# A two-path hybrid trunk step: sample inputs broadcast by transfers, the first chunk after a norm ordered by input tile, and a pair of heads moved into the step of two state reads

## The chip, the cores and the metric

One core of one Trainium2 chip runs the whole program as one launch. The metric is the device time of an execution in microseconds (us), the median of the runs. Engines: PE is TensorE, DVE is VectorE, ACT is ScalarE, POOL is GpSimd (here it only issues transfers), SP is SyncE (it issues the weight loads). All arithmetic is in fp32.

## What is computed

The reference runs one trunk of two layers for a prompt of 256 tokens and for 8 samples that each add one token; the kernel carries both as 264 columns. Layer 0 mixes by stick-breaking attention and retention, layer 1 by a gated state-space scan; after each mixer comes a layer norm, then a convolutional feed-forward part, then a layer norm. The parts that matter here, cut to their core:

```python
def _layer_norm(x, g, b):
    mu = jnp.mean(xf, axis=-1, keepdims=True)
    var = jnp.mean(jnp.square(xf - mu), axis=-1, keepdims=True)
    return ((xf - mu) * lax.rsqrt(var + LN_EPS) * g + b)
...
def _ssd_scan(x, dt, a, bm, cm, d_skip, h0):
    ...
    contrib = jnp.einsum('bcjgs,bcjge,bcjgep->bcgeps', bc, to_end, xf)
    def step(h, inp):
        return h * cd[..., None, None] + ct, h
    ...
    y = y + jnp.einsum('bcigs,bcige,bcgeps->bcigep', cc, jnp.exp(cum), h_start)
    y = y + d_skip.astype(jnp.float32)[:, :, None] * xf
```

For a sample the scan is one step: its state of a group (128 rows of the state by 8 heads x 64 = 512 channels) is multiplied by a decay for each head, and the outer product of B (128 values) and dt * x (512 values) is added; the new state is then read with C.

## The kernel before

**Products.** The weights come in 473 chunks of 1 MB (4 input tiles by 4 output tiles of 128 x 128), one after another through all phases. SP loads a chunk to `raw`; ACT copies it, rounded, to `hi` (line 553); DVE makes the rest, `lo = raw - hi` (line 563), each two chunks ahead of PE (`LOOK`); PE then makes three matmuls for each of the 16 blocks (lines 653 to 655: hi x xh, hi x xl, lo x xh), 48 for a chunk, each with 264 moving columns, into four accumulators `acc`. This stream of matmuls runs through the whole program; everything else that PE does is put between its pieces.

**Norms.** Three of four layer norms (l = 0, 1, 2) are followed by a phase that multiplies their result (up0, bc, up1). In the last chunk ahead of a norm PE sums, and then runs 12 unneeded matmuls (line 2381). DVE (`norm`) forms mean and variance, then centres four input tiles at once (`center`, line 1789, 128 x 1056), inverts the root that ACT made of the variance (lines 1172, 1810), and for each tile of 264 columns scales (`scale_tile`, line 1797) and, once ACT has rounded the tile to `xh` (line 1188), makes the rest `xl` (`low_tile`, line 1802). This is repeated for the four groups q of four tiles. PE starts chunk 0 of the next phase tile by tile (`x_first`, `x_lo`) with the output tile n as outer loop and the input tile k as inner loop; chunks 1, 2 and 3 wait for all four tiles of group 1, 2 and 3.

**The scan** runs beside the 64 chunks of the phase "ssd". Each chunk has four steps of 12 matmuls; a group g of 8 heads takes 28 steps (r = 0 to 27, 7 chunks), 8 groups in all, and tables give the step at which each piece of work is put behind the 12 matmuls, on PE and in the same order on DVE, ACT and POOL. Each engine works strictly in its order. The pieces are:
- at r = 22 PE turns the inputs of the samples of the next group (`group_samples`), DVE multiplies them by dt into `xtmp` (line 2046, 8 rows of 512), ACT rounds them and DVE makes the rest (line 2051), both into rows of `xdr`;
- `spread` at `SPREAD_AT` (r = 0, 2, 5, 7, 10, 12, 15, 17), one for each sample b: one matmul of 512 columns against a column of a selector (line 2426) that copies the row of sample b to 128 partitions of the bank `bank_spread`. DVE then adds it times B to the state (`renew`, line 1960). One bank serves all: the next spread waits for `state_new`, the renewal before;
- `read_state` for two samples at r = 5, 10, 15 and 20 (line 2440, 16 records for 8 matmuls of 8 x 128);
- `pair_heads` for two heads of the prompt at `PAIR_AT` = 4, 9, 14, 19 (lines 2459, 2461), which DVE adds to the result in the same step (line 1968). `DECAY_AT` and `WEIGHT_AT`, the steps of the preparations on ACT and DVE, are computed from `PAIR_AT`;
- at r = 20 also `group_cb` (lines 2485, 2486), at r = 26 and 27 turns and products of the prompt's inputs (lines 2103, 1985).

**POOL** issues the transfers of the scan in one fixed order. A unit u is the states of two samples in one group (512 KB, 32 units in all); for each u: load the state of u + 2 (line 843, which waits for the store of u - 1 to land and for its reads), load the decay rows of u + 2, broadcast to 128 partitions (line 835, which waits for ACT to have used the buffer), wait for both renewals of u, store the state (line 861).

## Time and profile before

| | |
|---|---|
| time before, median of 3 runs | 3062.95 us (3060.9 to 3064.45) |
| the profiled execution: its time, its span from first to last instruction | 3062.5 us, 3060.7 us |
| busy share of the span: PE, DVE, ACT, POOL | 99%, 65%, 53%, 4% |
| share of PE, DVE and ACT in the chain of work that ended last | 92%, 5%, 1% |
| HBM traffic over the span | 195 GB/s |
| mean granted TensorE clock | 0.996 of full |

Times in a trace are from the span's start. A row of the timeline gives the start, the time from the start of the first to the end of the last of its instructions, engine, line, operation and tiles, and in brackets the idle time of the engine ahead of it and what ended it. Matmuls overlap: each stands with some 0.28 us, but the next one starts 0.12 us later, so the cost of something on PE is read from starts. fp32 matmuls that are not of the rounded kind leave two records each.

### The profile page before, as it was taken

The page shows a single profiled execution, that of the slowest core. Times are in us where ns is not written, and L with a number is a line of the kernel's source. Part 1 is how long each engine was busy: PE and PEld are TensorE (multiplying, and loading weights), DVE is VectorE, ACT ScalarE, POOL GpSimd, SP SyncE. Part 2 cuts the span into 40 slices and gives each one's busy share as a digit, 9 for nine tenths or more (in the row PEclk, how much of TensorE's full clock was granted, in tenths as well). Part 3 has the DMA queues.
Part 4 walks back from the last instruction along what each step waited for, and adds up shares of the span by engine and source line. Part 5 has one row for each costly group of instructions (what it writes and reads, how often), then busy time and mean ns, then how long its engine had stood idle before and what let it go on. Part 6 is the DMA issues. An engine that isn't in the chain of part 4 may idle for free.

```text
span 3060.7 us, 60293 instructions
## 1 busy us (share of the span) xinstructions
PE 3016.8 (99%) x25089; PEld 2948.4 (96%) x25089; DVE 1985.3 (65%) x2512; ACT 1628.1 (53%) x1744; POOL 125.0 (4%) x222
## 2 busy tenths in 40 slices
PE   9999999999999999999999999999999999999997
PEld 9999899999999999999999999999999999999997
DVE  5455454677655666667758888777686566556665
ACT  4435575545444445445556767775454444445453
POOL 1010100000000000000000111100000000000000
PEclk9999999999999999999999999999999999999998
DMA  7565667544445445544456776665444544455452
GB/s 273 183 239 205 225 218 278 193 159 167 165 180 199 169 178 205 191 164 179 179 218 216 240 243 230 235 210 194 179 162 179 196 175 172 182 202 182 178 192 84
DMA packets 94523, 598.07 MB, mean 195 GB/s; under 512 B 11120, under 2 KB 11136, under 8 KB 33312
## 3 DMA queue, kind: packets, MB, share of 16 engines
q1 hardware_dynamic: 68688, 498.17, 44.0%
q0 software_dynamic: 25680, 97.69, 9.2%
q8 instruction: 115, 1.88, 0.2%
q14 instruction: 40, 0.33, 0.0%
HBM read 558.66 MB, written 37.15 MB: 195 GB/s over the span
## 4 chain that ended last, share of the span: by engine, by line
PE 92%; DVE 5%; ACT 1%; issue 1%; DMA 1%; DVEq 0%; POOL 0%; POOLq 0%; SPq 0%; ACTq 0%
PE acc L653 29%; PE acc L654 28%; PE acc L655 28%; DVE lo L563 1%; PE aux L2103 1%; PE aux L2426 1%; PE aux L2459 1%; PE aux L2440 1%; DVE x L1789 1%; DVE xl L1802 1%; DVE x L1797 1%; ACT xh L1188 0%; ACT hi L553 0%; PE aux L2188 0%; DMA x<-xsave 0%
## 5 line engine op out<-in xcount | busy, mean ns | idle before, releaser
L653 PE MATMUL acc<-xh,hi 128*128 128x264 f32 x7552 | 2174.8, 288 | 10.0 <-DVE lo L563 5.0
L654 PE MATMUL acc<-xl,hi 128*128 128x264 f32 x7552 | 2146.5, 284 | 0.0
L655 PE MATMUL acc<-xh,lo 128*128 128x264 f32 x7552 | 2139.0, 283 | 0.0
L653 PEld LDWEIGHTS acc<-xh,hi 128*128 128x128 f32 x7552 | 1422.9, 188 | 26.6 <-issue 13.9
L654 PEld LDWEIGHTS acc<-xl,hi 128*128 128x128 f32 x7552 | 1423.1, 188 | 4.2
L655 PEld LDWEIGHTS acc<-xh,lo 128*128 128x128 f32 x7552 | 1419.9, 188 | 0.0
L563 DVE TENSOR_TENSOR lo<-raw,hi 128x2048 fp32r<-128x2048 f32 x473 | 1077.7, 2287 | 381.2 <-ACT hi L553 380.5
L553 ACT ACTIVATE hi<-raw 128x2048 fp32r<-128x2048 f32 x473 | 897.6, 1907 | 492.6 <-DMA raw<-in_w 324.0
L552 ACT ACTIVATE xh<-pj 128x1056 fp32r<-128x1056 f32 x144 | 156.0, 1083 | 340.2 <-PE acc L655 279.6
L560 DVE TENSOR_TENSOR xl<-pj,xh 128x1056 fp32r<-128x1056 f32 x144 | 180.7, 1255 | 203.5 <-ACT hi L553 200.2
L1512 DVE SCALAR_TENSOR_TENSOR stage<-acc,par,stage 128x255 f32<-128x255 f32 x352 | 168.9, 480 | 23.1 <-DVE stage L1512 21.9
L901 ACT ACTIVATE stage<-acc,par 128x264 f32<-128x264 f32 x176 | 100.1, 571 | 133.8 <-PE acc L655 129.5
L935 ACT ACTIVATE pj<-acc 128x264 f32<-128x264 f32 x56 | 21.7, 389 | 78.7 <-PE acc L655 78.6
L1960 DVE SCALAR_TENSOR_TENSOR x<-aux,pj,x 128x512 f32<-128x512 f32 x64 | 47.8, 747 | 20.6 <-PE aux L2426 20.6
L911 ACT ACTIVATE small<-small 128x1 f32<-128x1 f32 x48 | 9.8, 203 | 89.5 <-DVE stage L1512 74.0
L1608 DVE SCALAR_TENSOR_TENSOR x<-x,aux 128x256 f32<-128x256 f32 x64 | 24.1, 418 | 50.2 <-PE aux L2188 50.2
L1845 DVE TENSOR_TENSOR pj<-stage 128x528 f32 (+1 forms) x44 | 31.2, 709 | 38.3 <-ACT stage L1199 38.3
L1428 DVE SCALAR_TENSOR_TENSOR x<-x,acc 128x264 f32 (+1 forms) x48 | 19.5, 426 | 43.9 <-PE acc L655 43.9
L1933 DVE SCALAR_TENSOR_TENSOR pj<-stage,par,pj 128x255 f32<-128x255 f32 (+2 forms) x96 | 46.2, 481 | 2.3
L808 POOL DMA_DIRECT2D out_fconv<-pj x2 | 1.1, 550 | 1049.4 <-DVE stage L1512 1049.4
L1951 DVE TENSOR_TENSOR x<-x,extra 128x512 f32<-128x512 f32 x64 | 43.7, 683 | 0.0
L1188 ACT ACTIVATE xh<-x,par 128x264 fp32r<-128x264 f32 x48 | 23.5, 512 | 30.7 <-DVE x L1797 30.7
(284 smaller groups left out, 1609.3 us busy)
## 6 DMA issues: line engine op xcount, KB each, us to landing
raw<-in_w SPq DMA_DIRECT2D x473, 1024.0 KB, 4.9
x<-in_ssm POOLq DMA_DIRECT2D x32, 512.0 KB, 4.4
out_ssms<-x POOLq DMA_DIRECT2D x32, 512.0 KB, 5.1
x<-in_ret POOLq DMA_DIRECT2D x16, 512.0 KB, 5.4
out_rets<-x POOLq DMA_DIRECT2D x16, 512.0 KB, 3.9
x<-in_ck POOLq DMA_DIRECT2D x16, 512.0 KB, 3.9
x<-in_cv POOLq DMA_DIRECT2D x16, 512.0 KB, 5.6
pj<-cumd POOLq DMA_DIRECT2D x32, 256.0 KB, 5.7
```

What stands on the lines that cost most here:

```text
L552: act.activation(xh[:, CK * s:CK * s + CK, :], src[:, CK * kc:CK * kc + CK, :], ACT.Copy)
L553: act.activation(hi[:, ph.hi(j), :], raw[:, r, :], ACT.Copy).then_inc(hi_done, 1)
L560: dve.tensor_tensor(xl[:, CK * s:CK * s + CK, :], src[:, CK * kc:CK * kc + CK, :], xh[:, CK * s:CK * s + CK, :].bitcast(F32), ALU.subtract)
L563: dve.tensor_tensor(lo[:, r, :], raw[:, r, :], hi[:, ph.hi(j), :].bitcast(F32), ALU.subtract).then_inc(lo_done, 1)
L653: pe.matmul(out, hi[:, s, w], xh[:, a, :], start=kc == 0 and k == 0, stop=False)
L654: pe.matmul(out, hi[:, s, w], xl[:, a, :], start=False, stop=False)
L655: m = pe.matmul(out, lo[:, r, w], xh[:, a, :], start=False, stop=kc == ph.kc - 1 and k == CK - 1)
L901: a(dst(q, n), acc[n][:, 0:T], ACT.Identity, bias=col(bias), scale=col(w))\
L1512: ins = stt(y[:, k:SEQ], h[:, 0:SEQ - k], one(w[:, width - 1 - k, :], n), y[:, k:SEQ], ALU.mult, ALU.add)
L1933: stt(y[:, k:SEQ], h[:, 0:SEQ - k], scw[:, 3 - k, t:t + 1], y[:, k:SEQ], ALU.mult, ALU.add)\
L1951: tt(v, v, cdbc[:, 8 * g:8 * g + 8, b].unsqueeze(2).to_broadcast([P, 8, HD]), ALU.mult)\
L1960: stt(v, bank_spread[:, :], pt[:, BM + g, SEQ + b:SEQ + b + 1], v, ALU.mult, ALU.add)\
```

## The change

Three edits. (1) In the scan, PE's 64 spread matmuls, ACT's rounding and DVE's rest of the inputs go. Instead `group_samples` makes four narrow matmuls that put the inputs of the 8 samples in four bands of 32 rows, DVE multiplies 104 rows of 128 by dt, POOL writes the four bands to a small array `xds` in HBM (`inputs_out`) and reads each sample's row of 512 back, broadcast to 128 partitions (`input_load`), into one of two SBUF buffers `xbc`; `renew` reads that buffer in place of the PSUM bank. (2) After the norms 0, 1 and 2 DVE centres the first four tiles one by one, and PE works chunk 0 with the input tile as outer loop; the first pass through the phase's loop is written out. (3) `PAIR_AT` moves by one step, to the steps of the reads.

```diff
-PAIR_AT = (4, 9, 14, 19)
+PAIR_AT = (5, 10, 15, 20)
...
-        xdr = hi[:, NHI - 1, 1536:2048]
+        xbc = [hi_end[:, 1536:2048], extra[:, 0:512]]
...
+            def first_chunk():
+
+                s, r = ph.hi(0), ph.raw(0)
+                pe.wait_ge(lo_done, ph.chunk0 + 1)
+                for k in range(CK):
+                    if k < CK - 1:
+                        pe.wait_ge(R["x_first"], (CK - 1) * (split - 1) + k + 1)
+                    else:
+                        pe.wait_ge(R["x_lo"], XB * split + 1)
+                    for n in range(CN):
+                        if k == 0:
+                            pe.wait_ge(drained, 4 * ph.panel0 + n + 1)
+                        w = slice((k * CN + n) * P, (k * CN + n + 1) * P)
+                        out = acc[n][:, 0:T]
+                        pe.matmul(out, hi[:, s, w], xh[:, k, :], start=k == 0, stop=False)
+                        pe.matmul(out, hi[:, s, w], xl[:, k, :], start=False, stop=False)
+                        m = pe.matmul(out, lo[:, r, w], xh[:, k, :], start=False, stop=False)
+                m.then_inc(used, 1)
...
-                    if pb == 0 and split is not None and (kc or not split):
+                    if pb == 0 and split is not None and (begun or not split):
...
+            elif split:
+                first_chunk()
+                body(Step(0), begun=True)
...
+            def inputs_out(g):
+
+                pool.wait_ge(R["misc_free"], MISC["st", g] + 1)
+                for t in range(4):
+                    pool.dma_start(d["xds"][NB * g:NB * g + NB, t * P:t * P + P], xtmp[32 * t:32 * t + NB, :])\
+                        .then_inc(R["xds_out"], 16)
+
+            def input_load(s):
+
+                if s % NB == 0:
+                    pool.wait_ge(R["xds_out"], 64 * (s // NB + 1))
+                if s >= 2:
+                    pool.wait_ge(R["state_new"], s - 1)
+                pool.dma_start(xbc[s % 2].unsqueeze(1), d["xds"][s:s + 1, :].partition_broadcast(P))\
+                    .then_inc(R[f"xbc_in{s % 2}"], 16)
...
+            inputs_out(0)
+            input_load(0)
+            input_load(1)
...
+                if u % 4 < 3:
+                    input_load(2 * u + 2)
                 pool.wait_ge(R["state_new"], 2 * (u + 1))
                 pool.dma_start(d["ssms"][u], hbuf[u % 3]).then_inc(R[f"state_out{u % 3}"], 16)
+                if u % 4 == 3 and u + 1 < units:
+                    inputs_out(u // 4 + 1)
+                    input_load(2 * u + 2)
+                if u + 1 < units:
+                    input_load(2 * u + 3)
...
-                    if r == ST_AT + 1 and -1 <= g < G - 1:
-                        act.wait_ge(R["misc_free"], MISC["st", g + 1] + 1)
-                        if g == -1:
-                            act.wait_ge(R["xdr_zero"], 1)
-                        else:
-                            act.wait_ge(R["spread"], 8 * g + 8)
-                        a(xdr[0:NB, :], xtmp[0:NB, :], ACT.Copy).then_inc(R["xdt_hi"], 1)
...
+                def center_tile(t):
+                    tt(x[:, t, :], x[:, t, :], lsum[:, :], ALU.add).then_inc(R["ln_fin"], 1)
+
+                if l == 3:
+                    center(0)
+                else:
+                    center_tile(0)
...
-                for q in range(XB):
+                scale_tile(0)
+                center_tile(1)
+                dve.wait_ge(R["ln_fin"], 8 * l + 3)
+                scale_tile(1)
+                low_tile(0)
+                center_tile(2)
+                low_tile(1)
+                dve.wait_ge(R["ln_fin"], 8 * l + 4)
+                scale_tile(2)
+                center_tile(3)
+                low_tile(2)
+                dve.wait_ge(R["ln_fin"], 8 * l + 5)
+                scale_tile(3)
+                low_tile(3)
+                for q in range(1, XB):
                     if q == XB - 1:
                         split_lo(dve, lead[l][3][0], Step(0), 3, None)
-                    if q:
-                        center(q)
-                        dve.wait_ge(R["ln_fin"], 5 * l + q + 2)
+                    center(q)
+                    dve.wait_ge(R["ln_fin"], 8 * l + 5 + q)
...
-                dve.wait_ge(R["spread"], 8 * g + b + 1)
+                dve.wait_ge(R[f"xbc_in{b % 2}"], 16 * (4 * g + b // 2 + 1))
                 dve.wait_ge(R["state_aged"], 8 * g + b + 1)
                 v = hbuf[u % 3][:, (b % 2) * 512:(b % 2) * 512 + 512]
-                stt(v, bank_spread[:, :], pt[:, BM + g, SEQ + b:SEQ + b + 1], v, ALU.mult, ALU.add)\
+                stt(v, xbc[b % 2], pt[:, BM + g, SEQ + b:SEQ + b + 1], v, ALU.mult, ALU.add)\
...
-                            dve.wait_ge(R["xdt_lo"], g + 1)
-                            dve.wait_ge(R["xdt_hi"], g + 1)
-                        tt(xtmp[0:NB, :].rearrange("p (h e) -> p h e", e=HD),
-                           dts[0:NB, 8 * g + 8:8 * g + 16].unsqueeze(2).to_broadcast([NB, 8, HD]),
-                           misc[0:NB, :].rearrange("p (h e) -> p h e", e=HD), ALU.mult).then_inc(R["misc_free"], 1)
-                    if r == XT_AT[0] and -1 <= g < G - 1:
-                        dve.wait_ge(R["xdt_hi"], g + 2)
-                        tt(xdr[32:32 + NB, :], xtmp[0:NB, :], xdr[0:NB, :].bitcast(F32), ALU.subtract)\
-                            .then_inc(R["xdt_lo"], 1)
+                            dve.wait_ge(R["xds_out"], 64 * (g + 1))
+                        tt(xtmp[0:104, :].rearrange("p (h e) -> p h e", e=HD),
+                           dts[0:104, g + 1, :].unsqueeze(2).to_broadcast([104, 2, HD]),
+                           misc[0:104, 0:P].rearrange("p (h e) -> p h e", e=HD), ALU.mult).then_inc(R["misc_free"], 1)
...
-            def spread(g, b):
-
-                pe.wait_ge(R["xdt_lo"], g + 1)
-                if g or b:
-                    pe.wait_ge(R["state_new"], 8 * g + b)
-                else:
-                    pe.wait_ge(R["sel_r"], 1)
-                mm(bank_spread[:, :], selr[0:72, b:b + 1].to_broadcast([72, P]), xdr[0:72, :],
-                   start=True, stop=True).then_inc(R["spread"], 1)
...
-                    m = turn(misc[0:NB, t * P:t * P + P], pt[:, XS + 4 * g + t, SEQ:T])
+                    m = mm(misc[32 * t:32 * t + NB, 0:P], pt[:, XS + 4 * g + t, SEQ:T], ident, start=True, stop=True)
...
-                        if r == SPREAD_AT[b]:
-                            spread(g, b)
```

**DVE, norm 0.** The first row below is the variance; line 1789 centres, 1797 scales, 1802 makes the rest. Before:

```order
L1781 SCALAR_TENSOR_TENSOR pj<-aux,pj 128x264
L1789 TENSOR_TENSOR x<-x,lsum 128x1056
L1810 RECIPROCAL pj<-pj 128x264
L1797 SCALAR_TENSOR_TENSOR x<-x,par,pj 128x264 x2
L1802 SCALAR_TENSOR_TENSOR xl<-x,par,xh 128x264
L1797 SCALAR_TENSOR_TENSOR x<-x,par,pj 128x264
L1802 SCALAR_TENSOR_TENSOR xl<-x,par,xh 128x264
L1797 SCALAR_TENSOR_TENSOR x<-x,par,pj 128x264
L1802 SCALAR_TENSOR_TENSOR xl<-x,par,xh 128x264 x2
L1789 TENSOR_TENSOR x<-x,lsum 128x1056
```

The same place now, where line 1847 centres one tile, 1827 four, 1835 scales and 1840 makes the rest:

```order
L1847 TENSOR_TENSOR x<-x,lsum 128x264
L1854 RECIPROCAL pj<-pj 128x264
L1835 SCALAR_TENSOR_TENSOR x<-x,par,pj 128x264
L1847 TENSOR_TENSOR x<-x,lsum 128x264
L1835 SCALAR_TENSOR_TENSOR x<-x,par,pj 128x264
L1840 SCALAR_TENSOR_TENSOR xl<-x,par,xh 128x264
L1847 TENSOR_TENSOR x<-x,lsum 128x264
L1840 SCALAR_TENSOR_TENSOR xl<-x,par,xh 128x264
L1835 SCALAR_TENSOR_TENSOR x<-x,par,pj 128x264
L1847 TENSOR_TENSOR x<-x,lsum 128x264
L1840 SCALAR_TENSOR_TENSOR xl<-x,par,xh 128x264
L1835 SCALAR_TENSOR_TENSOR x<-x,par,pj 128x264
```

Ahead of the second group there are now eleven instructions behind the reciprocal, three more than before, and one narrow centring ahead of it in place of a wide one.

**PE, one group of the scan, r = 0 to 10.** "..." stands for the rows of the stream (lines 653 to 655, now 669 to 671). Before, with spread on line 2426, the pair on 2459 and 2461, the read on 2440:

```order
L2426 MATMUL aux<-hi,selr 128x512
...
L2426 MATMUL aux<-hi,selr 128x512
...
L2459 MATMUL aux<-raw,x 64x256 x2
L2461 MATMUL aux<-raw,x 64x128 x2
L2103 MATMUL aux<-cons,extra 128x128
...
L2440 MATMUL aux<-x,raw 8x128 x8
L2426 MATMUL aux<-hi,selr 128x512
...
L2426 MATMUL aux<-hi,selr 128x512
```

The same steps now, with the turn on line 2160, the read on 2490 and the pair on 2509 and 2511:

```order
L2160 MATMUL aux<-cons,extra 128x128
...
L2490 MATMUL aux<-x,raw 8x128 x8
L2509 MATMUL aux<-raw,x 64x256 x2
L2511 MATMUL aux<-raw,x 64x128 x2
```

The spreads are gone, and the pair has moved from its own step to stand right behind the read.

**POOL, the same part.** Line 855 loads decay rows, 863 a state, 902 stores one, 878 is the new broadcast load:

```order
L902 DMA out_ssms<-x 128x1024
L878 DMA extra<-xds 128x512
L863 DMA x<-in_ssm 128x1024
L855 DMA pj<-cumd 128x512
L878 DMA hi_plain<-xds 128x512
```

Before, the order was the same without the two rows of line 878; at the end of a group four small stores `xds<-pj` now stand ahead of the next two such loads.

## Rows read from the trace of the kernel before

**Rows 1.** A window: length, busy PE, PEld, DVE, ACT, POOL, clock, DMA share, GB/s
```profile
1700.00:1750.00 50.00, 50.00 (x443) 45.95 (x442) 39.97 (x62) 33.84 (x46) 5.88 (x11) 1.00 0.70 248
```

**Rows 2.** Timeline of PE, scan, group 1 and the last read
```profile
1693.38 0.28 PE L655 MATMUL acc<-xh,lo 128*128 128x264 f32 x1
1693.60 0.62 PE L2440 MATMUL aux<-x,raw 128*8 128x128 f32 x16
...
1694.49 0.28 PE L653 MATMUL acc<-xh,hi 128*128 128x264 f32 x1
...
1697.40 0.40 PE L2426 MATMUL aux<-hi,selr 72*128 72x512 f32 x1
1697.64 0.29 PE L653 MATMUL acc<-xh,hi 128*128 128x264 f32 x1
...
1702.45 0.65 PE L2459 MATMUL aux<-raw,x 128*64 128x256 f32 x4
...
1703.25 0.39 PE L653 MATMUL acc<-xh,hi 128*128 128x264 f32 x1
...
1724.16 0.62 PE L2440 MATMUL aux<-x,raw 128*8 128x128 f32 x16
...
1725.39 0.36 PE L653 MATMUL acc<-xh,hi 128*128 128x264 f32 x1
...
2053.27 0.62 PE L2440 MATMUL aux<-x,raw 128*8 128x128 f32 x16
2053.82 0.39 PE L653 MATMUL acc<-xh,hi 128*128 128x264 f32 x1
```

**Rows 3.** Waits of PE: who for whom, total us, times, longest
```profile
PE aux L2103 <- DVE hi_plain L1985: 1.4, 4, 0.4
PE aux L2426 <- DVE x L1960: 1.2, 1, 1.2
```

**Rows 4.** Timeline of DVE in the scan: inputs of group 1, two renewals
```profile
1674.71 0.67 DVE L2046 TENSOR_TENSOR extra<-pj,aux 8x512 f32<-8x512 f32 x1 [1.15 <-PE aux L2103]
...
1685.96 0.74 DVE L1960 SCALAR_TENSOR_TENSOR x<-aux,pj,x 128x512 f32<-128x512 f32 x1
...
1705.99 0.75 DVE L1960 SCALAR_TENSOR_TENSOR x<-aux,pj,x 128x512 f32<-128x512 f32 x1 [0.41 <-PE aux L2426]
```

**Rows 5.** Timeline of POOL, one issue of decay rows in the scan
```profile
1698.63 0.54 POOL L835 DMA_DIRECT2D pj<-cumd  x1 [0.19 <-issue]
```

**Rows 6.** The tile cumd: 33 transfers, from issue to landing
```profile
DMA to landing us min/median/max: 2.0/5.7/8.0
```

**Rows 7.** Timeline of PE behind norm 0: chunks 0, 1 and 3
```profile
692.41 0.36 PE L653 MATMUL acc<-xh,hi 128*128 128x264 f32 x1 [0.41 <-DVE xl L1802]
...
699.77 0.36 PE L653 MATMUL acc<-xh,hi 128*128 128x264 f32 x1 [0.16 <-DVE xl L1802]
...
712.10 0.36 PE L653 MATMUL acc<-xh,hi 128*128 128x264 f32 x1 [0.45 <-DVE xl L1802]
```

**Rows 8.** Timeline of DVE, norm 0
```profile
687.70 1.25 DVE L1789 TENSOR_TENSOR x<-x,lsum 128x1056 f32<-128x1056 f32 x1
688.86 1.80 DVE L1810 RECIPROCAL pj<-pj 128x264 f32<-128x264 f32 x1
690.69 0.90 DVE L1797 SCALAR_TENSOR_TENSOR x<-x,par,pj 128x264 f32<-128x264 f32 x2
691.77 0.49 DVE L1802 SCALAR_TENSOR_TENSOR xl<-x,par,xh 128x264 fp32r<-128x264 f32 x1 [0.18 <-ACT xh L1188]
...
694.47 1.25 DVE L1789 TENSOR_TENSOR x<-x,lsum 128x1056 f32<-128x1056 f32 x1
```

**Rows 9.** Timeline of ACT, norm 0: the root of the variance
```profile
687.81 0.52 ACT L1172 ACTIVATE pj<-pj,small 128x264 f32<-128x264 f32 x1 [1.85 <-DVE pj L1781]
```

**Rows 10.** Two windows in the attention part, columns as in rows 1
```profile
473.00:475.00 2.00, 0.37 (x16) 0.08 (x4) 1.97 (x3) 0.00 (x0) 0.41 (x1) 1.00 1.00 399
477.00:479.00 2.00, 2.00 (x11) 2.00 (x11) 0.00 (x0) 0.92 (x2) 0.53 (x1) 0.50 1.00 348
```

49 lines of the change are left out of this document (27 added, 22 removed).

## The prediction

> **What bounds the kernel now.** I read first the page's busy shares and the chain that ended last (table above): PE is busy 99% of the span and holds 92% of the chain. Then a window in the middle of the scan [rows 1]: PE 50.00 us of 50.00, DVE 39.97, ACT 33.84, the transfer engines at a share of 0.70. So in the scan every nanosecond that PE spends beside the stream of chunk matmuls is paid in full, and DVE and the transfers have some room, of a fifth to a third. Then the starts on PE around each piece of work beside the stream [rows 2], and last the three norms, which are the only places in these phases where PE waits for DVE again and again [rows 7].
>
> **Spreads.** A stream matmul starts 0.12 us after the one before. A spread alone moves the next stream matmul by 0.24 (1697.40 to 1697.64) [rows 2]. A read with a spread behind it costs 1693.38 to 1694.49, 1.11 less the usual 0.12, so 0.99; a read alone costs 0.55 from its start, and 0.10 more because such a block starts 0.22 after the last stream row and not 0.12, so 0.65 [rows 2]. A spread behind a read is thus 0.34. Of 64 spreads 24 stand behind a read (r = 5, 10, 15 in 8 groups) and 40 do not: 24 x 0.34 + 40 x 0.24 = 17.8 us off PE.
>
> **Waits that go with them.** One spread waited 1.2 us for the renewal ahead of it, because one bank serves all; four turns at r = 26 waited 1.4 us together for DVE's products [rows 3], which stand right behind the rest (line 2051) that the change removes. Both go: 2.6 us. I count them whole; the lower end is nothing, if other waits come in their place.
>
> **Pairs.** A pair alone costs 0.80 + 0.10 = 0.90 [rows 2]. No row shows a pair behind a read. The nearest is `group_cb` behind a read, with the same 256 and 128 moving columns: 1.23 + 0.10 = 1.33 for both, so 0.68 for the second piece [rows 2]. I take 0.68, since what is saved is entering and leaving the stream once instead of twice: 32 x 0.22 = 7.0 us. The lower end is nothing saved. The Trainium skill ("TensorEngine Tiling (Array Packing)", Key Properties) speaks against this edit: a change of tiling mode drains the engine, and the read (8 columns wide) and the pair (64 wide) are different modes. By that rule the join saves less than 7.0, perhaps nothing; the row of the read with `group_cb` is also a change of mode and shows 0.68, so I go by the row.
>
> **What PE gets instead.** Eight times four turns become four narrow matmuls. Their nearest row is a read, which has eight such and costs 0.65; four cost between half of that and all of it, and what the turns cost today comes off. I take 0.1 us net for each group, 0.8 us; the ends are -2 and +3 us. The turn that shared the pair's old step now stands alone, which is in the same bounds.
>
> Scan, on PE: -17.8 - 2.6 - 7.0 + 0.8 = -26.6 us.
>
> **The broadcasts by transfer** cost PE nothing while they land in time. POOL's issues take 0.54 us each [rows 5], and a broadcast of 256 KB, like the decay rows, lands 5.7 us after its issue in the median and 8.0 at the most [rows 6]. At the head of a group the inputs are made at 1674.71 and the first renewal runs at 1685.96 [rows 4]: 11.2 us. Needed: 0.3 for the product, 4 x 0.54 for the stores, 2.0 for a small store to land (the least in rows 6 is the one store among them), and 5.7: 10.2. That leaves 1 us in the median, and is 1.3 too late at 8.0. Inside a group the load for an even sample can be issued right behind the decay rows, at 1698.63 + 0.54 = 1699.17, and is wanted at 1705.99 [rows 4, 5]: 6.8 us, against 5.7 and something for standing behind the decay rows. At r = 0 the decay load itself moves one step later with `PAIR_AT`, and takes this load along. So some renewals will be late by 0 to 2 us. What is queued behind them is DVE's own work: the next ageing, a pair's result, and `lo` of a chunk two chunks ahead. DVE has 10 of 50 us free and loses its waits for spreads, so I cost this at 0 for PE; the upper end, 0.4 us in each of 32 units, is 13 us. The 64 loads are 17 MB in some 430 us, 39 GB/s on top of 248 [rows 1], so the share of 0.70 becomes about 0.81; the weights keep their place five chunks ahead.
>
> **The norms.** Here the edit works against itself. DVE, by [rows 8, 9]: the wide centring starts at 687.70 and the reciprocal at 688.86, the first scaling at 690.69, 1.83 after the reciprocal. A narrow centring takes between 0.31 (a quarter of 1.25) and 0.41 (two scalings take 0.90, one 0.49); I take 0.35. It would let the reciprocal start at 688.05, but the root on ACT ends at 687.81 + 0.52 = 688.33. So the first scaling starts at 690.2, 0.5 us earlier. From there to the wide centring of group 1 there were eight instructions in 694.47 - 690.69 = 3.78 us; now there are eleven: 3.28 for the eight at 0.41, 1.05 for three centrings, and 0.9 of waits, mostly of the last rest, which cannot start before 1.08 after its scaling (690.69 to 691.77) as ACT must round between. That is 5.2 to 5.4, so group 1 starts at about 695.55, 1.1 us later than today, and so do groups 2 and 3, which are unchanged. On PE [rows 7]: chunk 0 starts at some 692.1 instead of 692.41 and, with no gaps, is through at 697.9 instead of 699.6. But chunk 1 waits for group 1 today already (0.16 us at 699.77), and chunk 3 for group 3 (0.45 at 712.10). Both now come 1.1 us later: chunk 1 at 700.9, after 2.8 us of idle PE, and chunk 3 at 713.2 (PE by itself would be there at 700.9 + 11.9 = 712.8, so DVE still decides). The gain in chunk 0 is lost in front of chunk 1, and what is left is 1.1 us more for each of three norms: +3.3. Ends: 0 and 1.5 for each.
>
> **The clock.** In the attention part PE was busy for only 0.37 of 2.00 us, and soon after ran at a granted clock of 0.50, 1.2 instead of 2.4 GHz, with 11 matmuls in 2 us where 16 start otherwise [rows 10]. The new idle stretch of 2.8 us behind each norm is longer than that one. A fall costs at least the 0.9 us of work lost in those 2 us, at most perhaps twice that; I take 1.5, of which the 0.4 that chunk 3 has in hand comes off: 1.1 us. I count one fall in three norms, +1.1; ends 0 and 4.5. The Trainium skill ("TensorE: Matmul & The Clock Gate", HAM oscillation) says the same of gaps between bursts of matmuls: the engine returns to half clock. [...]
>
> **The sum.** -26.6 + 3.3 + 1.1 = -22.2 us. The profiled execution has a span of 3060.7 and a time of 3062.5; it becomes 3038.5 and 3040.3. The median of the runs lies 0.45 above its time, so I forecast 3041 us.
>
> **Rivals.**
> - *The join of pair and read saves nothing*, because the engine drains between them: 3041 + 7 = 3048. For it speaks only that no row shows that pair of widths. 0.08.
> - *Late inputs reach PE.* Available times of 6.8 us against 5.7 to 8.0 speak for it, DVE's room against. With a third to all of the 13 us: 3045 to 3054. 0.13.
> - *The norms gain.* If the rests of group 1 came no later than today, chunk 0's earlier end would take off the 0.16 and the 0.45 that PE waits and no clock would fall: -26.6 - 2, so 3035. Against it stands the count of instructions. 0.08.
> - *Slower.* The place is the load for the even samples. It stands behind the state load, which waits for the landing of a store, which waits for the renewal; if a broadcast from the new array lands late, the whole ring turns slower than PE. PE must lose 22 + 6 = 28 us more, 0.9 in each of 32 units, on top of the 6.8 us that are available and some 3 us that DVE and the reads at the end of a unit can take: a landing of 10.7 us in the median decides, against 5.7 (at most 8.0) for the same size today [rows 6]. It would give 3069 and more. 0.06.
> - *The edits cancel, or do not do what they say* (the spreads' columns were hidden, say): within 6 us of 3063. Against it, PE is busy 50.00 of 50.00. 0.04.
>
> The forecast itself has 0.61, with its own range of 3037 to 3045. A measurement of this kernel tells 0.2%, 6 us, from no change. Faster by more: 0.61 + 0.08 + 0.13 + 0.08 = 0.90; within it 0.04; slower 0.06. The range of 3036 to 3050 leaves out the slower case, the cancelling, the worse half of the late inputs and part of the gaining norms.
>
> **What would show it.** Right: no wait of PE for `renew`; a read with its pair from some 1.3 us, at r = 20 some 2.0; chunk 1 behind each norm waiting 2.5 to 3 us for line 1840, chunk 3 some 1.1 us later against the norm's start; renewals waiting 0 to 2 us for the new loads, above all at r = 5; a granted clock of 0.50 behind one norm or two. Wrong: PE waiting in the scan for reads or `lo` behind late renewals; a read with its pair at 1.55; group 1 of a norm starting less than 0.5 us later than now. What would make it wrong most easily is the landing time of the broadcasts, which no row shows for this array.

## The result and the profile after

The changed kernel takes 3072.11 us, the median of 10 runs (3069.87 to 3076.58). The kernel before, run beside it, takes 3064.37 (10 runs, 3060.9 to 3067.14). The ratio is 1.003, with an interval of 1.0022 to 1.0038: slower by 8 us, where 3041 us, 22 less than before, was forecast. The profiled execution has a span of 3072.1, against 3060.7.

From the page of the changed kernel: PE's part of the busy shares, the software queue (packets, MB, share), and three kinds of issues with their size and the median from issue to landing.

```profile
PE 3004.4 (98%) x25064; PEld 2942.2 (96%) x25064; DVE 1978.6 (64%) x2517; ACT 1621.1 (53%) x1733; POOL 174.8 (6%) x317
...
q0 software_dynamic: 31824, 114.61, 11.1%
...
x<-in_ssm POOLq DMA_DIRECT2D x32, 512.0 KB, 6.4
out_ssms<-x POOLq DMA_DIRECT2D x32, 512.0 KB, 7.7
...
pj<-cumd POOLq DMA_DIRECT2D x32, 256.0 KB, 6.4
```

PE lost a percent of its busy share. The window that [rows 1] shows of before, with the same columns, and two short ones behind the first norm:

```profile
700.00:702.00 2.00, 0.21 (x2) 0.24 (x3) 1.82 (x5) 1.71 (x5) 0.00 (x0) 1.00 0.86 287
702.00:704.00 2.00, 2.00 (x11) 2.00 (x11) 1.79 (x4) 1.36 (x4) 0.00 (x0) 0.51 0.58 242
1700.00:1750.00 50.00, 47.49 (x428) 44.12 (x427) 36.57 (x61) 34.17 (x45) 11.17 (x22) 0.97 0.81 266
```

In the scan PE was busy 50.00 of 50.00 before; now it idles for 2.5 of 50 us, and the granted clock of 0.97 says that it ran at 1.2 GHz and not at 2.4 for a part of them. The share of the transfers is 0.81, as forecast. So PE has become a waiting engine. For what, the waits tell (engine, tile and line of the waiting instruction, what released it: us in total, times, the longest). First PE's in the changed kernel, then DVE's:

```profile
PE aux L2509 <- DVE raw L2005: 14.6, 16, 3.4
PE acc L669 <- DVE xl L1840: 8.3, 3, 2.8
PE aux L2490 <- DVE x L2022: 6.6, 9, 1.2
```

```profile
DVE x L2022 <- DMA hi_plain<-xds: 46.9, 13, 6.2
...
DVE x L2022 <- DMA extra<-xds: 14.5, 7, 3.0
```

Before, PE waited 0.2 us for a pair's weights and 1.2 for a renewal in the whole scan; now it waits 14.6 for weights (line 2005), 6.6 for renewals (2022). DVE's renewals wait 61.4 us for the broadcast inputs, 20 times. Only the third group, 8.3 us for `xl`, is of the norms.

One such event from beginning to end. POOL, changed kernel, start and length of each issue (878 is a broadcast of inputs, 855 decay rows, 863 a state load, 902 a state store):

```profile
1690.75 0.57 POOL L878 DMA_DIRECT2D hi_plain<-xds  x1 [4.34 <-DMA xds<-pj]
1691.31 0.55 POOL L878 DMA_DIRECT2D extra<-xds  x1
1691.85 0.53 POOL L863 DMA_DIRECT2D x<-in_ssm  x1
1697.95 0.54 POOL L855 DMA_DIRECT2D pj<-cumd  x1 [5.57 <-ACT raw L1362]
1698.48 0.54 POOL L878 DMA_DIRECT2D hi_plain<-xds  x1
```

DVE, at the other end of the last of these:

```profile
1705.92 0.75 DVE L2022 SCALAR_TENSOR_TENSOR x<-hi_plain,pj,x 128x512 f32<-128x512 f32 x1 [5.09 <-DMA hi_plain<-xds]
...
1707.73 1.51 DVE L1995 SCALAR_TENSOR_TENSOR pj<-stage,par,pj 128x255 f32<-128x255 f32 x3
1709.16 2.29 DVE L563 TENSOR_TENSOR lo<-raw,hi 128x2048 fp32r<-128x2048 f32 x1
1711.37 0.55 DVE L2005 TENSOR_TENSOR raw<-raw 128x384 f32<-128x384 f32 x1
1711.84 0.75 DVE L2022 SCALAR_TENSOR_TENSOR x<-extra,pj,x 128x512 f32<-128x512 f32 x1
...
1714.08 0.55 DVE L2005 TENSOR_TENSOR raw<-raw 128x384 f32<-128x384 f32 x1
```

And PE, with the read on 2490 and the pair on 2509:

```profile
1711.46 0.41 PE L2490 MATMUL aux<-x,raw 128*8 128x128 f32 x8
1712.64 0.41 PE L2490 MATMUL aux<-x,raw 128*8 128x128 f32 x8 [0.77 <-DVE x L2022]
1714.78 0.65 PE L2509 MATMUL aux<-raw,x 128*64 128x256 f32 x4 [1.74 <-DVE raw L2005]
```

The buffer came free when the renewal of 1694.68 had read it, at some 1695.4, but POOL stood from 1692.4 to 1697.95 at the issue of the decay rows, which waits for ACT (5.57 us). The broadcast was issued behind it at 1698.48 and landed 7.4 us later. DVE stood 5.09 us, and when it went on it had its whole order before it: the convolution's products (line 1995), a `lo` of 2.29 us, the pair's first weights, the next renewal and, at 1714.08, the pair's second weights. PE, 6.7 us after the late renewal, waits for the next one (0.77) and then for those second weights (1.74).

The norms behave as forecast. PE at chunk 1 behind norm 0, in the changed kernel (to be set beside [rows 7]):

```profile
698.73 0.28 PE L650 MATMUL acc<-xh,lo 128*128 128x264 f32 x1
701.79 0.36 PE L669 MATMUL acc<-xh,hi 128*128 128x264 f32 x1 [2.78 <-DVE xl L1840]
```

The window above from 702 shows the granted clock of 0.51 behind this idle stretch. The same pair of idle and fall stands behind all three norms (idle 2.78, 2.77 and 2.76 us at 701.79, 1486.91 and 2279.75).

To see where time went I cut each profiled span at PE's starts, at the last unneeded matmul ahead of the norms 0, 1 and 2 and at the start of the scan: up to norm 0, from there to norm 1, the part of dt, the scan with the output projection, and what follows norm 2. The labels are those of the experiments below; each row is one profiled execution. In us, with PE's idle time in the scan:

```
                     span    to n0   n0..    dt     scan   n2..    idle in scan
before              3060.7  691.6   783.4   96.7   691.3  797.7    6.2
changed             3072.1  692.5   785.1   98.3   694.6  801.7   24.0
e1 norms alone      3067.1  691.9   785.3   98.3   691.5  800.1    6.5
e2 pair alone       3060.1  691.7   783.3   96.7   690.7  797.7    6.0
e3 broadcasts alone 3060.1  690.4   783.3   96.7   691.1  798.7   18.5
e5 changed, by ACT  3045.0  692.1   785.1   98.3   670.2  799.4    6.9
e6 e3, by ACT       3051.2  692.5   783.4   96.6   681.0  797.7    9.9
e9 e6 and pair      3038.7  691.0   783.3   96.7   670.0  797.7    6.7
e10 one load first  3054.4  690.4   786.3   97.8   680.1  799.9   12.5
e11 loads unread    3043.7  691.4   784.6   99.5   667.7  800.5    4.7
e12 e3 and pair     3065.6  689.0   783.5   96.7   697.7  798.7   22.7
e13 POOL reordered  3053.5  692.1   784.9   98.1   678.3  800.1   11.8
```

### The profile page after: what moved, and what is told of

It reads as the page before. It is cut to its first block, busy times and chain, and to the rows that moved or that the text cites. A ratio compares the mean times of both kernels' runs of the same rounds, so it can differ in the third digit from the quotient of the medians.

```text
span 3072.1 us, 60119 instructions
## 1 busy us (share of the span) xinstructions
PE 3004.4 (98%) x25064; PEld 2942.2 (96%) x25064; DVE 1978.6 (64%) x2517; ACT 1621.1 (53%) x1733; POOL 174.8 (6%) x317
## 3 DMA queue, kind: packets, MB, share of 16 engines
q0 software_dynamic: 31824, 114.61, 11.1%
## 4 chain that ended last, share of the span: by engine, by line
PE 85%; DVE 6%; DMA 6%; issue 2%; ACT 1%; POOL 0%; DVEq 0%; POOLq 0%; SPq 0%; ACTq 0%
PE acc L669 27%; PE acc L670 27%; PE acc L671 26%; DMA extra<-xds 2%; DMA hi_plain<-xds 1%; DVE lo L563 1%; DMA out_ssms<-x 1%; DMA xds<-pj 1%; DVE x L2022 1%; PE aux L2160 0%; DVE pj L1995 0%; DVE x L2013 0%; DVE raw L2005 0%; PE aux L2245 0%; ACT hi L553 0%
## 5 line engine op out<-in xcount | busy, mean ns | idle before, releaser
L981 ACT ACTIVATE pj<-acc 128x264 f32<-128x264 f32 x56 | 21.7, 389 | 78.7 <-PE acc L671 78.6
L2022 DVE SCALAR_TENSOR_TENSOR x<-hi_plain,pj,x 128x512 f32<-128x512 f32 x32 | 24.0, 750 | 47.2 <-DMA hi_plain<-xds 46.9
L1361 ACT ACTIVATE raw<-pj,x 128x256 f32<-128x256 f32 x64 | 32.2, 503 | 23.7 <-DVE raw L2005 23.7
```

The source lines that it names most:

```text
L2022: stt(v, xbc[b % 2], pt[:, BM + g, SEQ + b:SEQ + b + 1], v, ALU.mult, ALU.add)\
```

## Experiments

Two theories stood at the start. **Late inputs** (theory L of the first texts below): the spreads' time did leave PE, and was lost again because renewals wait for the broadcasts. **Slack** (theory P; later texts name theirs anew): the pair's new step, or the traffic on the transfer engines, is what costs. The edits were first run one by one. A ratio is to the kernel before as run beside that experiment, whose median went from 3063.25 to 3064.53 us, with an interval of 95% behind it; so differences between medians of two experiments are good to about 1 us at best.

**e1_norm**: only the edit at the norms.

```diff
-                center(0)
+                if l == 3:
+                    center(0)
+                else:
+                    center_tile(0)
...
+            elif split:
+                first_chunk()
+                body(Step(0), begun=True)
```

> The kernel before with edit 2 alone (narrow centrings, chunk 0 by input tile). Theory L (the scan loses to late input loads, the norms cost what the trace of the changed kernel shows: 2.8 us of idle PE behind each of three norms and a fall of the clock after each): 5 to 6.5 us slower than before, three falls of the clock. Theory P (the scan loses to the moved pair, with the norms as here): the same. If the norms were not the cause of their share: within 1 us of before.

Measured: 3068.88 us, ratio 1.0021 (1.0012 to 1.003), 5.6 us slower. Windows of e1_norm behind its three norms, columns as above:

```profile
702.00:704.00 2.00, 2.00 (x12) 2.00 (x12) 1.78 (x5) 1.01 (x3) 0.00 (x0) 0.55 0.21 86
1487.00:1489.00 2.00, 2.00 (x13) 2.00 (x12) 1.79 (x4) 1.33 (x4) 0.00 (x0) 0.57 0.43 176
2276.00:2278.00 2.00, 1.78 (x8) 1.81 (x9) 1.96 (x4) 1.36 (x4) 0.00 (x0) 0.50 0.75 315
```

The clock is at half speed, 1.2 GHz, behind every norm: three falls in this execution, where one was counted.

**e2_pair**: only `PAIR_AT`.

```diff
-PAIR_AT = (4, 9, 14, 19)
+PAIR_AT = (5, 10, 15, 20)
```

> The kernel before with edit 3 alone (pair moved into the step of the reads, spreads kept). Theory L: the pair costs about 0.8 behind a read where it cost 0.9 alone, so 0 to 3 us faster, no waits of PE for line 1943. Theory P (the pair in the reads' step has too little time behind its weights on DVE, and this makes PE wait): 10 us slower or more.

Measured: 3062.67 us, ratio 1.0 (0.9991 to 1.001); the scan 0.6 us shorter and no new wait. The pair's step costs nothing as long as the inputs come from spreads.

**e3_bcast**: only the broadcasts, issued by POOL.

```diff
-                        if r == SPREAD_AT[b]:
-                            spread(g, b)
...
+                if u % 4 < 3:
+                    input_load(2 * u + 2)
```

> The kernel before with edit 1 alone (inputs broadcast by transfers). Theory L: PE waits some 15 to 25 us in the scan behind renewals that wait for their load, which eats the 18 us of the spreads: between 5 us faster and 5 us slower than before. Theory P: the loads are hidden, 15 to 20 us faster.

Measured: 3061.86 us, ratio 0.9998 (0.9988 to 1.0007). Renewals wait 33.6 us for loads, 18 times, and PE's first row of waits is

```profile
PE aux L2469 <- DVE raw L1965: 15.4, 10, 2.7
```

So already alone this edit gives back all that the spreads cost, and the row is the pair's weights, not the reads.

**e4_noload**: the changed kernel with 62 of the 64 broadcast loads left out; every renewal reads the inputs of the first two samples, so the states of the samples are other numbers.

```diff
                 if s >= 2:
                     pool.wait_ge(R["state_new"], s - 1)
+                    return
...
-                dve.wait_ge(R[f"xbc_in{b % 2}"], 16 * (4 * g + b // 2 + 1))
+                dve.wait_ge(R[f"xbc_in{b % 2}"], 16)
```

> The changed kernel without 62 of its 64 broadcast loads: every renewal reads the inputs of the first two samples (so the sample states and what follows from them are other numbers); the small stores to HBM and all waits of POOL stay. Theory L: PE's 21 us of waits in the scan and the three falls of the clock there go, 25 us faster than the changed kernel, some 17 us faster than before. Theory P: no more than 5 us faster than the changed kernel, PE still waits for the weights of line 2005.

Measured: 3052.46 us, ratio 0.9969 (0.9956 to 0.9981), 19.7 below the changed kernel, where 25 was expected. The run takes three things away together: DVE's waits, POOL's issues and the traffic. The next ones part them. It also has something of its own: at 2062.56, the end of the scan, PE stands 3.8 us for a `lo`, because DVE has waited 6.06 us for the reload of `xsave`. In e11 below that wait of DVE is 2.35 us, and e11, which does issue the loads, is 7 us faster than e4. So 19.7 is a lower bound of what late loads cost.

**e5_actq**: the changed kernel with the stores of the inputs and the broadcasts issued by ACT, at fixed steps. **e6_actq_old**: the same, but with the norms and the pair's step as before.

```diff
-                pool.dma_start(xbc[s % 2].unsqueeze(1), d["xds"][s:s + 1, :].partition_broadcast(P))\
+                act.dma_start(xbc[s % 2].unsqueeze(1), d["xds"][s:s + 1, :].partition_broadcast(P))\
...
+                    if r == ST_AT + 1 and -1 <= g < G - 1:
+                        inputs_out(g + 1)
+                    if r == ST_AT + 3 and -1 <= g < G - 1:
+                        input_load(NB * (g + 1))
+                        input_load(NB * (g + 1) + 1)
+                    if 0 <= g < G:
+                        for b in range(2, NB):
+                            if r == SPREAD_AT[b - 2] + 1:
+                                input_load(NB * g + b)
```

> The changed kernel with the small stores and the 64 broadcast loads issued by ACT, at fixed steps of the scan (stores at r = 23, the first two loads of a group at r = 25, the others one step after the renewal that frees their buffer), in place of POOL. Theory Q (the loads are late because they stand in POOL's order and its queue, behind state loads and stores of 512 KB): they land 3.5 to 5 us after the issue, PE's waits in the scan fall from 21 to under 8 us, 12 to 20 us faster than the changed kernel. Theory B (the extra traffic itself makes every transfer late): landings stay above 6 us and the time within 5 us of the changed kernel.

> The kernel before with edit 1 alone (norms and the pair's step as before), stores and loads on ACT as in the run before this. Theory Q: the scan as there, and 6 us less for the norms: 15 to 20 us faster than the kernel before. Theory B: within 3 us of the kernel before.

Measured: e5 3046.83 us, 0.9946 (0.9932 to 0.9959), 25.3 below the changed kernel; e6 3051.18 us, 0.9962 (0.9948 to 0.9976), 13 below the kernel before. In e5 renewals wait 6.1 us in 4 places, and the loads land in 5.6 us in the median. Theory Q has the direction and misses its numbers: 3.5 to 5 us for the landing, 12 to 20 us for e5, 15 to 20 for e6. Two windows of e5 in the scan, the first with the columns as above, the second with PE's alone (length, busy PE, clock, DMA share, GB/s):

```profile
1700.00:1750.00 50.00, 47.76 (x440) 44.40 (x440) 39.36 (x63) 36.75 (x47) 6.92 (x13) 1.00 0.83 284
...
1900.00:1950.00 50.00, 50.00 (x462) 1.00 0.86 296
```

PE still idles for 2.2 us in the first of them, but only for 6.9 in the whole scan, and the clock stays at 2.4 GHz. Where nothing is late it starts 462 matmuls in 50 us, against 443 before [rows 1]. The traffic is higher than in the changed kernel, 284 and 296 GB/s against 266. The bytes are not what costs.

**e7_kmajor**: of the norms' edit only PE's half, chunk 0 with the input tile outside, DVE's order as before. **e8_filler**: the whole norms' edit, with six matmuls behind chunk 0 whose result nobody reads.

```diff
                 m.then_inc(used, 1)
+                for _ in range(6):
+                    pe.matmul(aux[3][:, 0:2 * P], ones, cons[:, :], start=True, stop=True)
```

> The kernel before with PE's half of edit 2 alone: chunk 0 with the input tile as outer loop and the first pass written out, DVE's norm as it was. If DVE's longer order is what delays chunks 1 and 3: the same time as before, chunk 1 behind norm 0 at the same distance from the warm matmuls, about 1.3 us of idle PE in front of it, no fall of the clock. If PE's order itself costs: 3 to 6 us slower.

> The kernel before with edit 2 and 6 unneeded matmuls (256 columns, fp32, some 2.6 us) behind chunk 0 of each of the three phases, in what was idle time of PE. If the falls of the clock behind the norms are real costs and come from the idle stretch: no falls there, and 2 to 4 us faster than with edit 2 alone, so 3 to 4 us slower than before. If they cost nothing: 6 us slower than before, as with edit 2 alone.

Measured: e7 3064.4 us, 1.0003 (0.9993 to 1.0012). e8 3066.47 us, 1.001 (1.0 to 1.0019), with this window of e8_filler behind norm 0:

```profile
702.00:704.00 2.00, 2.00 (x19) 2.00 (x18) 1.99 (x5) 1.15 (x3) 0.00 (x0) 1.00 0.00 0
```

Behind the norms 1 and 2 the clock is 1.00 too. Without the idle stretch there is no fall, and 2.4 us less is lost than in e1, or 3.3 if each is taken against the kernel before beside it. So the three falls cost some 0.8 to 1.1 us each, and the rest of the loss is put down to DVE's longer order, since PE's half alone costs nothing that can be told; DVE's half alone was not run.

**e9_best**: the version that these point to, e6 with the pair in its new step.

```diff
-PAIR_AT = (4, 9, 14, 19)
+PAIR_AT = (5, 10, 15, 20)
```

> The kernel before with the broadcasts issued by ACT and the pair in the step of the reads; the norms as before. Theory A (the pair's new step saves 0.09 us for each of 32 by the join, as its own run and the rows of the changed kernel show, and no more): the part with the scan goes from 681.0 us in the run of the broadcasts by ACT alone to about 678, the time from 3051.2 to about 3048. Theory B (once the spreads are gone, the pair in the same step also takes away idle stretches and a fall of the clock, so that the part with the scan is what it was in the run of all edits by ACT): 670 us, and with the old norms, which are about 4 us cheaper, a time of some 3041 us.

Measured: 3040.38 us (3039.55 to 3041.48), ratio 0.9923 (0.9909 to 0.9936): 24 us faster than before, 32 than the changed kernel. The waits of PE for weights are small again:

```profile
PE aux L2486 <- DVE raw L1982: 3.4, 5, 1.2
```

Theory B holds, in its numbers, and theory A's 0.09 us for each join is too little; where the 10.8 us that part e9 from e6 come from is told further down.

**e10_poolfirst**: the changed kernel, with POOL issuing, but the even sample's broadcast first in its unit.

```diff
+                if u % 4 < 3:
+                    input_load(2 * u + 2)
                 if u + 2 < units:
                     if u >= 1:
                         state_load(u + 2)
                     decay_load(u + 2)
-                if u % 4 < 3:
-                    input_load(2 * u + 2)
```

> The changed kernel with one line of POOL's order moved: in each unit of a pair of samples, the broadcast for the next even sample is issued ahead of the state load (which waits for a store to land) and of the decay rows. Theory O (the broadcasts are late because POOL is held at that wait when their buffer comes free): renewals wait for them less, from 20 waits and 61 us to under 8 waits and 20 us, PE's idle in the scan from 24 to about 10 us, and the time from 3072 to about 3060. Theory Q (the software queue itself lands them late, whatever their order; the gain came from the queue of ACT): waits and time about as in the changed kernel, 3068 to 3074 us.

Measured: 3058.31 us (3050.7 to 3065.32, 11 runs), ratio 0.9983 (0.9974 to 0.9992): 14 us from the order of one issue. The time is that of theory O, its numbers for DVE are not: 24 waits, 34.0 us. DVE's waits by buffer in e10, against 46.9 and 14.5 in the changed kernel:

```profile
DVE x L2022 <- DMA extra<-xds: 25.9, 18, 4.7
DVE x L2022 <- DMA hi_plain<-xds: 8.1, 6, 3.3
```

The even samples (`hi_plain`) are in time inside a group now; 6.3 of their 8.1 us are at its head. The odd ones (`extra`) still stand behind a store of 512 KB, and with the even ones in time their own lateness shows.

**e11_unread**: the changed kernel with every broadcast issued by POOL, but neither waited for by DVE nor read, except for the last two; the renewal takes the state itself in place of the inputs, so its numbers are others. POOL instead waits for the landing of a buffer's last load before it issues the next.

```diff
+                    pool.wait_ge(R[f"xbc_in{s % 2}"], 16 * (s // 2))
...
-                dve.wait_ge(R[f"xbc_in{b % 2}"], 16 * (4 * g + b // 2 + 1))
+                if g == G - 1 and b >= NB - 2:
+                    dve.wait_ge(R[f"xbc_in{b % 2}"], 16 * (4 * g + b // 2 + 1))
...
-                stt(v, xbc[b % 2], pt[:, BM + g, SEQ + b:SEQ + b + 1], v, ALU.mult, ALU.add)\
+                stt(v, v, pt[:, BM + g, SEQ + b:SEQ + b + 1], v, ALU.mult, ALU.add)\
```

> The changed kernel, all 64 broadcasts issued on POOL as there, but the renewals don't wait for them and take the state itself in place of the inputs (so the computation is changed there; the operation has the same size). POOL waits for the landing of a broadcast before it reuses its buffer. Theory W (the loss is the wait of DVE for late inputs, and what stands behind it in DVE's order): about as the run without those broadcasts, 3052 to 3056 us, PE's idle in the scan about 10 us. Theory T (the loss is what the broadcasts do to POOL's order and to the other transfers, so that state loads, decay rows or weights are late without any wait for the inputs): 3062 us or more, with DVE waiting for decay rows or states.

Measured: 3045.32 us, ratio 0.9936 (0.9922 to 0.995), 26.8 below the changed kernel. The loads land even later than there (median 7.1 us, at most 13.2), POOL waits longer for stores (161.0 us against 129.3), and hardly anything of it reaches PE, whose waits for weights are now

```profile
PE aux L2511 <- DVE raw L2006: 2.1, 4, 0.7
```

Theory W has the cause and misses its number, 3052 to 3056 us, by 7 us: it was taken from e4. Theory T falls. With the issues, the order and the traffic all in place, the loss is gone, so what the broadcasts cost is DVE's waiting for them and the work that stands behind it.

**e12_pool_oldnorm**: the changed kernel with the old norms. **e13_poolorder**: POOL's order in a unit written anew, both broadcasts first, then the store, the decay rows, and the state load last.

```diff
                 if u % 4 < 3:
                     input_load(2 * u + 2)
+                    input_load(2 * u + 3)
                 pool.wait_ge(R["state_new"], 2 * (u + 1))
                 pool.dma_start(d["ssms"][u], hbuf[u % 3]).then_inc(R[f"state_out{u % 3}"], 16)
...
+                if u + 2 < units:
+                    decay_load(u + 2)
+                    if u >= 1:
+                        state_load(u + 2)
```

> The changed kernel with its norms left as in the kernel before; the broadcasts stay with POOL. Theory N (the norms' cost of 4 to 6 us adds to whatever the scan does): 3066 to 3068 us, with PE's idle in the scan near the 24 us of the changed kernel. Rival (PE's later start into the scan, 1.6 us behind the norm, is what puts DVE and the transfers out of step, so that the norms' edit costs more here than alone): under 3063 us and an idle of 15 us or less.

> The changed kernel with POOL's order per unit written anew: both broadcasts first (each right when its buffer comes free), then the state store, then the decay rows, and the state load, which waits for a store to land, last. Theory O2 (all of the lateness is POOL being held when a buffer comes free): the renewals' waits fall to about 10 us, PE's idle in the scan to some 7 us, and the time to that of the same kernel with ACT issuing, 3045 to 3048 us. Theory L (the software queue also lands them about 1 us later, 6.5 us in the median against 5.6, and the state load moves into the place of what is late): it stays near the run with one broadcast first, 3055 to 3060 us.

Measured: e12 3068.23 us, ratio 1.0019 (1.001 to 1.0028), idle in the scan 22.7: theory N, the norms add 3.9 us to what this scan takes. Its renewals wait 64.0 us, nearly twice the 33.6 of e3, from which it differs by the pair's step alone:

```profile
DVE x L1982 <- DMA hi_plain<-xds: 47.2, 16, 6.5
...
DVE x L1982 <- DMA extra<-xds: 16.8, 9, 4.4
```

e13: 3053.5 us, ratio 0.9971 (0.996 to 0.9981). In e13 the waits and the landing are

```profile
DVE x L2022 <- DMA hi_plain<-xds: 15.1, 8, 3.9
...
DVE x L2022 <- DMA extra<-xds: 1.4, 2, 1.2
```

that is 16.5 us in all against 61.4. Over the 64 loads the median landing is 5.5 us, against 6.4 in the changed kernel and 5.6 in e5 by ACT's queue. So theory L falls on the landing: POOL's queue lands as fast as ACT's once its order is right. O2 falls on the size: 18.6 of some 25 us come back. What is left is partly in the head of a group. In the changed kernel, e10 and e13 the first loads wait for four small stores (POOL stands there for 37.2 us in 8 groups in the changed kernel), and e13's two largest waits, 2.9 and 3.9 us, are at a group's first renewal.

## Why the prediction was wrong, step by step

**The step that failed** is "DVE has 10 of 50 us free and loses its waits for spreads, so I cost this at 0 for PE; the upper end, 0.4 us in each of 32 units, is 13 us". Three things were wrong in it.
- *The cover.* I named what is queued behind a late renewal as the next ageing, a pair's result and a `lo` two chunks ahead. The pair's weights (line 2005) and the read of the very state stand there too, and both are wanted at once. PE waited 14.6 and 6.6 us for these two, and hardly for `lo`. DVE's free fifth is an average and does not help: DVE works in order, and the 5 us that it stands at 1700 are followed by 6 us of work that it cannot do side by side.
- *The lateness.* I had "0 to 2 us". It was 61.4 us in 20 waits, 3.1 each and at most 6.2. The landing was 6.4 us in the median and 11.2 at most, where [rows 6] had 5.7 and 8.0 with 17 MB less on the same queue (97.69 against 114.61). More weighs when the issue comes: from the start of the renewal that frees a buffer to the issue it is 1.6 us in the median, but over 2.5 in 16 of 48 and up to 7.1, because POOL stands at the decay rows or at a state load that waits for a store to land. I had seen both and priced neither for the inputs. With one issue moved ahead only 2 of 48 are over 2.5.
- *The size at PE.* The scan with its projection is 24.4 us longer than in e5: 17.1 are idle time, 5.0 are three falls of the clock (in windows of 50 us its grant is 0.97 at 1650, 1700 and 1850), and 2.3 are pieces of work that cost more when PE has waited in them.

These numbers come from all starts of PE in the scan, where the stream's own matmuls take the same time in each kernel. A piece is what stands between two of them; where a fall touches it, what it takes over the mean of its kind is put under falls. Idle time has its shortest gaps in it here. In us:

```
             idle   falls   pieces   stream and ends
before        6.4     0.0    113.3   571.6
changed      24.1     5.0     93.9   571.6
e2            6.0     1.9    111.2   571.6
e3           18.6     4.3     96.6   571.6
e5            7.0     0.0     91.6   571.6
e6           10.0     1.5     97.8   571.7
e9            6.8     0.0     91.6   571.6
e12          22.7     9.7     93.6   571.7
```

**The slower rival** had the right place, "a landing of 10.7 us in the median decides", and the wrong condition. It took 6.4, since the hold of POOL comes on top of the landing, and since DVE and the reads did not take the 3 us that were counted on.

**Spreads and join, 26.6 us.** In e9, where little is late, the scan part is 21.3 us shorter than before. Of the 5.3 that are missing, 3.0 are the waits: 2.6 were to go, and idle time is 0.4 longer instead, because 3.4 us of waits for a pair's weights came in their place. That was the stated lower end. The other 2.3 are in the pieces, 21.7 us less where the sum has 17.8 + 7.0 - 0.8 = 24.0.

The term that was mis-sized there is the spread behind a read. The prediction counts a piece up to the first stream matmul behind it. First a read with its pair in the changed kernel. Then, in the kernel before, the end of a read with a spread, and the last stream matmul ahead of a pair alone and of a read alone [rows 2] with the second one behind it:

```profile
1821.61 0.28 PE L671 MATMUL acc<-xh,lo 128*128 128x264 f32 x1
1821.82 0.62 PE L2490 MATMUL aux<-x,raw 128*8 128x128 f32 x16
1822.37 0.65 PE L2509 MATMUL aux<-raw,x 128*64 128x256 f32 x4
...
1823.17 0.39 PE L669 MATMUL acc<-xh,hi 128*128 128x264 f32 x1
1823.40 0.28 PE L670 MATMUL acc<-xl,hi 128*128 128x264 f32 x1
```

```profile
1694.15 0.50 PE L2426 MATMUL aux<-hi,selr 72*128 72x512 f32 x1
1694.49 0.28 PE L653 MATMUL acc<-xh,hi 128*128 128x264 f32 x1
1694.61 0.28 PE L654 MATMUL acc<-xl,hi 128*128 128x264 f32 x1
```

```profile
1702.23 0.28 PE L655 MATMUL acc<-xh,lo 128*128 128x264 f32 x1
...
1703.48 0.29 PE L654 MATMUL acc<-xl,hi 128*128 128x264 f32 x1
...
2053.06 0.28 PE L655 MATMUL acc<-xh,lo 128*128 128x264 f32 x1
...
2054.05 0.28 PE L654 MATMUL acc<-xl,hi 128*128 128x264 f32 x1
```

Behind a pair or a read the second stream matmul starts 0.23 after the first, and only then every 0.12 (1823.17, 1823.40); behind a spread it is 0.12 at once (1694.49, 1694.61). So I count to the second one and take off 0.24, two starts of the stream. A read with a spread is 0.98 us in the mean over the scan, a read alone 0.75, a pair alone 1.00, a read with its pair 1.55. A spread behind a read was thus worth 0.23 and not 0.34, 2.6 us over 24 of them. The join saves 0.20, 6.4 us over 32, and its 7.0 were nearly right. By the prediction's own measure, to the first one, it looks like half of that, 1.44 us against 0.65 + 0.90.

With a spread between read and pair, as in e2, the three cost 1.98, against 0.98 + 1.00: there the join saves next to nothing, but for r = 20, where no spread stands.

The Trainium skill ("TensorEngine Tiling (Array Packing)", Key Properties) says that a change of tiling mode drains the engine. The rows show no such price between these two widths, as 0.20 of the 0.22 are saved; whether the two widths are two modes, no run here shows.

**Pair's step.** There is more in that edit than the join, and the prediction did not see it. With inputs in time it gains 10.8 us (e6 to e9), in the scan of the profiled executions 11.0: 6.2 in the pieces, nearly all of it the join, 3.2 of idle time, and 1.5 for a fall of the clock (0.97 in the window from 1700) that e9 has not. With late inputs it costs 6.4 us (e3 to e12, 3061.86 to 3068.23): the pieces give 3.0 us, but idle time is 4.1 and the falls are 5.4 us more, and the renewals' waits go from 33.6 to 64.0. `PAIR_AT` also moves the decay rows by a step, with the broadcasts behind them, but this does not show as a reason: from the renewal that frees a buffer to the issue it is over 2.5 us in 18 of 48 cases in e3 and in e12. What shows is that DVE comes to the samples 2 and 4 of a group sooner after that renewal, in the mean 7.0 and 7.9 us in e12 against 8.0 and 8.8 in e3.

**Norms, 3.3 + 1.1 us.** Right in the mechanism: an idle stretch of 2.8 us ahead of chunk 1 was forecast and is 2.78. The price was 5.6 us alone (e1), 3.9 in the changed kernel (e12 to it) and 6.4 between e9 and e5. The price of a fall, 1.1 us, holds within what e8 can tell (0.8 to 1.1); its count does not, three and not one.

Taken together, 25 of the 31 us between forecast and measurement are the late inputs. With the same three edits and the broadcasts issued by ACT (e5) the kernel takes 3046.83, 5.8 over the forecast. The fastest version, e9, leaves out the norms' edit, for which the forecast would have been 3041 - 4.4 = 3036.6; it takes 3040.38.

## What to carry to other kernels

When a broadcast moves from an engine to a transfer, write down for each buffer the moment it comes free, everything that its issuing queue waits for between that moment and the issue, and what the waiting engine has behind it in its own order. Do not count its free time on average as cover: here 10 of 50 us free covered little of the waits, and the price was set by the first things in its order that the bounding engine wanted soon. Put such loads ahead of any issue that waits for a landing, or on a queue that waits for nothing else, before judging whether the transfer pays.

## What the runs showed of the hardware

- A load's landing depends on its place in its queue more than on which engine issues it. Broadcasts of 256 KB by POOL landed in 6.4 us in the median (at most 11.2), in 5.5 (9.0) with POOL's order changed, and in 5.6 (8.9) by ACT. The Trainium skill ("DMA: Bandwidth & Descriptors", Issuing engine by pattern) gives plain loads to the hardware queues as generally faster. For the kernel this agrees, 3046.83 against 3072.11 us, yet 18.6 of those 25 us come back on POOL's queue too.
- Four small stores ahead of a reload kept POOL waiting 37.2 us in 8 groups, 4.7 us each, where 2.0 was taken from a single quiet store [rows 6].
- An idle stretch of PE is not followed by a fall of the clock every time. Behind the norms of the seven kernels with the norms' edit and no filler (the changed kernel, e1, e4, e5, e10, e11, e13) there are 21 such stretches of 2.8 us, and a granted clock of 0.5 behind 17 of them. Behind the other four, two in e10 and one each in e4 and e11, it stays 1.00. A stretch of 1.8 us ahead of the scan, at 1591, has a clock of 0.50 behind it in e2 and e7 and of 1.00 in the kernel before. So a count of falls from a single trace has some luck in it.
- In the scan, where PE sets the time, a fall costs 1.5 us in e6, 1.7 in the changed kernel (5.0 for three), 1.9 in e2 and 2.2 in e3 (4.3 for two).
- The stream of matmuls with 264 columns takes up its pitch of 0.12 us one matmul late behind a read or a pair (8 and 64 stationary columns; 0.23, then 0.12), and at once behind a spread (1694.49, 1694.61).
